# Layer 1's memory gate stored turned, its values product swapped, and the projections of the shared stage reordered

## The chip, the cores and the metric

The kernel runs on one core of one Trainium2 chip. The metric is the device time of one execution in microseconds (us); three runs of the kernel before gave 2721.72, 2722.89 and 2724.37 us, median 2722.89. The engines are named as the profile names them: PE (TensorE matmuls; PEld its weight loads), DVE (VectorE), ACT (ScalarE), POOL (GpSimd) and SP (the queue that issues most DMAs).

## What is computed

One inference step of a two-layer decoder trunk over 2048 prompt rows and 8 sample rows, all in float32 (D = 1024, four heads of 128 in every attention). Layer 0 mixes a gated short convolution with a memory attention. Layer 1 mixes a dilated window attention of three groups with a memory attention. The parts of layer 1 that the change touches:

```python
z = rms_norm(x, norm_g) @ w_in
qd, gd, mq, mg = jnp.split(z, [...])                 # 3 queries of 512, gate 512, memory query 512, memory gate 512
dil_out = dil_fn(qd).reshape(b, t, D_DIL) * jax.nn.silu(gd)
q = rms_norm(mq.reshape(b, t, MEM_HEADS, HEAD_DIM), mem_q_g) * (HEAD_DIM ** -0.5)
mem_out = mem_attend(q, mem_kv).reshape(b, t, D_MEM) * jax.nn.silu(mg)
out = jnp.concatenate([dil_out, mem_out], axis=-1) @ w_out
return x + out
```

`mem_attend` is a softmax over 256 memory rows followed by the product with the memory's values. The keys and values of the three dilation groups (`shared_kv`) are one projection of x, with a norm on the keys.

## The kernel before

Every large matrix product is made of three PE products of split operands (`split3`, lines 128 to 132: high by high, high by low, low by high), so a 128x512 result tile over eight chunks of 128 takes 24 matmuls. A transpose ("turn") is a matmul against the identity into PSUM.

The stages run in this order: the first mixing stage of layer 0 (`mix_stage`), its attention and output stage (`out_stage` with `conv` true), the projections of layer 1 (`shared_stage`), the dilated attention (`dil_stage`), and the output stage of layer 1 (`out_stage` again, `conv` false). Each engine executes its own list in order; semaphores carry the dependences. The lists are written out by hand, one function per engine.

**shared_stage** makes twelve blocks of 512 channels: key and value of three groups, three queries, the memory query, and two gates (block 4 is gd, block 5 is mg). The two blocks in `first` are made one after the other by plain products, one 128-token tile per step (lines 1455 to 1471 on PE). In the first of them ACT takes squares for the norm and DVE scales. In the second, ACT only copies the tile out of PSUM (line 1124), while ACT and DVE also make sums of x that the rest needs (`recombine`, `sums`, `sums_low`, `sums_high`). The other ten blocks are made as five pairs with seven half-size products in place of eight. Kinds of blocks: "norm" (four squares and a root on ACT, a reciprocal and four scalings on DVE), "copy" (nothing beyond DVE's addition) and "silu" (a sigmoid on ACT, a multiplication on DVE). Before, `first` is key(0), value(0), and the last pair is gate(4), gate(5). PE may run three tiles ahead of the engines that empty PSUM.

**out_stage, layer 1** works through 16 tiles of 128 tokens. In step t, PE runs: `values(t-1)` (16 products of probabilities and values), `turn_query(t)`, `right_end(t-2)` (12 matmuls), `scores(t)` (12 matmuls of 256 columns), `turn_o(t-1)`, `left(t-1)` (24 matmuls; the last 12 need the low half of the attention output, `olo_done`), sample gathers, `turn_probs(t)`, `turn_mix(t)`, `right_begin(t-1)`. The attention output comes as token rows: `gate` multiplies by the inverse row sum and by the gate in four DVE instructions (line 3543), `turn_o` transposes, ACT and DVE split the result (`high_o` line 3370, `low_o` line 3550).

DVE in step t: `joint_max(t)` (lines 3493, 3495), `query_low(t)` (3604), `gate(t-1)`, `add_right`, `maxima(t)` (3608, 3611), `weights(t)` (3508 to 3516), `low_o`, `combine(t)` (eight instructions of line 3527, one of 3531), the reciprocal `invert(t)` (3621), `add_left`, `probs_second(t)` (3630), `mix_low(t)` (3616), and in steps 3 to 10 additions for the sample rows (`join`, 2872 and 2875). ACT in step t: `group_weights(t)` (3405), `query_high(t)` (3434), a weighing of cached values for a sample row (`weigh`, 2801), `high_o`, two exponentials (3399), `weighted_sum(t)` (four instructions of 3394), two exponentials, another `weigh`, `probs_first(t)` (3361), `mix_high(t)` (3413). `weighted_sum(t)` waits for `weights(t)`, `scores(t)` for `query_low(t)`, which waits for `query_high(t)`.

Layer 0's `out_stage` has the turned form already: its gate is stored as channels by tokens, its values product gives turned rows, and the probabilities are scaled before they are transposed (line 3625).

Of the kernel before, what the change touches and what calls it, by code (L numbers as in the profile page):

```python
# [25 lines left out]
ALU = mybir.AluOpType  # L26
# [672 lines left out]
def shared_stage(core, block, stack, lead, prep, first, pairs, ops, bufs, xt_hi, xt_lo, xs, zero, spare, w_out, keys, opening):  # L699
# [22 lines left out]
    for blk in first:  # L722
        for i in range(SAMPLES):
            outs.append((blk.kind, P if i < NT else S, blk.dst[i * P:i * P + (P if i < NT else S), :], 0))
# [85 lines left out]
    with ExitStack() as st:  # L810
# [205 lines left out]
        def _(act):  # L1016
# [85 lines left out]
            for b in range(2):  # L1102
                for i in range(SAMPLES):
# [17 lines left out]
                    else:  # L1121
                        if i == 0:
                            act.wait_ge(o_done, SAMPLES)
                        act.activation(row, product, ACT.Copy).then_inc(o_done, 1)
# [47 lines left out]
        def _(dve):  # L1172
# [140 lines left out]
            for b in range(2):  # L1313
                for i in range(SAMPLES):
# [66 lines left out]
        def _(pe):  # L1381
# [61 lines left out]
            for b in range(2):  # L1443
                for i in range(SAMPLES):
# [12 lines left out]
                    for k in range(KD):  # L1457
# [4 lines left out]
                        if i == NT:  # L1462
                            sample_product(out % 4, xs[:, k, 0:LOW], wh[b].bitcast(F32)[:, k, :], k == 0, False)
                            m = sample_product(out % 4, xs[:, k, 0:LOW], wl[b].bitcast(F32)[:, k, :], False, k == KD - 1)
                        else:
# [1701 lines left out]
def out_stage(core, block, layer, src, x, y, ops_in, x_s, y_s, keys, front=None, remains=None, follow=None, closing=None):  # L3167
# [28 lines left out]
    with ExitStack() as st:  # L3196
# [20 lines left out]
        else:  # L3217
# [5 lines left out]
            def cat(low, u):  # L3223
# [4 lines left out]
                 "scored maxed biased exped inverted pturned first_done second_done summed og_done oturned ohi_done "  # L3228
                 "olo_done mhi_done mlo_done left_done right_done left_added right_added")
        (q_in0, q_in1, g_in0, g_in1, x_in0, x_in1, m_in0, m_in1, y_out0, y_out1, qturned, qhi_done, qlo_done,  # L3230
         scored, maxed, biased, exped, inverted, pturned, first_done, second_done, summed, og_done, oturned, ohi_done,
# [10 lines left out]
        if conv:  # L3242
            fresh, evened = core.sems(st, f"{tag}_fresh", "fresh evened")
            own = own + dec.sems + keys.sems + [fresh, evened]
            renewed = core.sb(st, f"{tag}_renewed", [P, 1])
# [19 lines left out]
        def _(sp):  # L3265
            def load(t):
# [20 lines left out]
                if conv:  # L3287
                    sp.dma_start(g_b[:, u, :].rearrange("p (h t) -> p h t", t=P),
                                 src["mg_t"].rearrange("(h p) t -> p h t", p=P)[:, :, rows]).then_inc(g_in[u], 16)
                else:  # L3290
                    sp.dma_start(g_b[:, u, :], src["mg"][rows, :]).then_inc(g_in[u], 16)
# [66 lines left out]
        def _(act):  # L3358
# [4 lines left out]
            def high_o(t):  # L3363
                if conv:
                    act.wait_ge(og_done, t + 1)
                    of = og[:, :].rearrange("p (h t) -> p h t", t=P)
                else:
                    act.wait_ge(oturned, t + 1)
                    of = turned_heads
# [66 lines left out]
            def step(t):  # L3436
# [3 lines left out]
                if not conv and t > 1:  # L3440
                    group_weights(t)
                if conv or t > 1:
# [45 lines left out]
        def _(dve):  # L3488
# [31 lines left out]
            def combine(t):  # L3520
                u = t % 2
                dve.wait_ge(od_begun, t + 1)
                for g in (1, 2):
# [7 lines left out]
                dve.tensor_tensor(od[:, :], od[:, :], gd_b[:, u, :], ALU.mult).then_inc(ops, 1)  # L3531

            def gate(t):
# [4 lines left out]
                if conv:  # L3538
                    dve.tensor_tensor(og[:, :], ps[:, 3, :], g_b[:, u, :], ALU.mult).then_inc(og_done, 1)
                    return  # L3540
                for h in range(H):
                    cols = slice(h * HD, (h + 1) * HD)
                    m = dve.scalar_tensor_tensor(out=og[:, cols], in0=sums[:, h, :], scalar=stat[:, 3, h:h + 1],
                                                 in1=g_b[:, u, cols], op0=ALU.mult, op1=ALU.mult)
                m.then_inc(og_done, 1)

            def low_o(t):
                dve.wait_ge(ohi_done, t + 1)
                of = og[:, :].rearrange("p (h t) -> p h t", t=P) if conv else turned_heads
# [68 lines left out]

            def invert(t):
                dve.wait_ge(exped, t + 1)  # L3620
                dve.reciprocal(stat[:, 3, :], stat[:, 2, :]).then_inc(inverted, 1)
                if conv:
                    dve.wait_ge(inverted, t + 1)
                    for h in range(H):
                        m = dve.tensor_scalar(prob[:, h, :], prob[:, h, :], stat[:, 3, h:h + 1], None, ALU.mult)
                    m.then_inc(evened, 1)
# [5 lines left out]
            def first():  # L3632
# [4 lines left out]
                else:  # L3637
                    joint_max(1)
# [8 lines left out]
            def step(t):  # L3647
# [16 lines left out]
                if not conv and t > 1:  # L3664
                    weights(t)
# [4 lines left out]
                else:  # L3670
                    combine(t)
# [43 lines left out]
        def _(pe):  # L3715
# [13 lines left out]
            def values(t):  # L3729
# [13 lines left out]

            def turn_o(t):

                pe.wait_ge(og_done, t + 1)
                turn(og).then_inc(oturned, 1)
# [21 lines left out]
            def turn_probs(t):  # L3769
                pe.wait_ge(evened if conv else exped, t + 1)  # L3770
# [43 lines left out]
            def first():  # L3814
# [9 lines left out]
                else:  # L3824
                    pe.wait_ge(mlo_done, 1)
                    project(0, 0, range(MIX))
                turn_probs(0)
# [505 lines left out]
```

## Time and profile before

| | |
|---|---|
| median of three runs | 2722.89 us (2721.72 to 2724.37) |
| the profiled execution | 2719.55 us, span 2717.4 us |
| PE busy | 2702.2 us, 99% of the span |
| DVE busy | 1789.1 us, 66% |
| ACT busy | 1112.9 us, 41% |
| chain that ended last | PE 93%, DVE 4% |
| PE clock | full in all 40 slices |
| layer 1's output stage | about 2432 to 2717 us of the span |

The span is the profiled time of the core's program; 2.2 us lie around it. "Busy" of PE counts overlapping matmuls as one stretch, so a share of 99% says that something is in the array nearly always, not how fast it runs there. A line number names the instruction's source line in the kernel.

### The profile page before, as it was taken

The numbers are of one execution on the slowest core, as the hardware profiler recorded it, in microseconds if no ns is written. First come the engines' busy times: TensorE is split into PE (matmuls) and PEld (weight loads), VectorE is DVE, ScalarE is ACT, GpSimd is POOL, SyncE is SP. The second block draws the span as 40 slices with busy tenths as digits, with TensorE's granted clock in tenths as the row PEclk, the third lists the DMA queues.
The fourth block names the chain that finished last, engine by engine and source line by source line (L and its number), as shares of the span: only waits on it lengthen the run. The fifth ranks groups of instructions, "written<-read, shape, count | busy, mean of one in ns | idle before, by whom it ended". The sixth has DMA issues, their size and how long they took to land.

```text
span 2717.4 us, 41295 instructions
## 1 busy us (share of the span) xinstructions
PE 2702.2 (99%) x14834; PEld 2259.7 (83%) x14834; DVE 1789.1 (66%) x3925; ACT 1112.9 (41%) x3346; POOL 383.1 (14%) x610
## 2 busy tenths in 40 slices
PE   9999999999999999999999999999999999999999
PEld 7788888888887888878888888888888889998887
DVE  7686766768678644435575667877674767777764
ACT  7533131212326234225434353532332349876632
POOL 0101010100101000000112032333424223210000
PEclk9999999999999999999999999999999999999999
DMA  8486555655676734324266676787768789757642
GB/s 281 143 250 208 183 167 179 207 182 171 210 246 207 222 115 156 101 97 152 94 246 228 211 268 216 274 284 264 247 237 284 262 311 330 231 177 262 217 154 82
DMA packets 292628, 567.75 MB, mean 209 GB/s; under 512 B 32432, under 2 KB 91760, under 8 KB 292424
## 3 DMA queue, kind: packets, MB, share of 16 engines
q1 hardware_dynamic: 257032, 462.31, 52.0%
q0 software_dynamic: 35392, 102.80, 10.6%
q8 instruction: 118, 1.93, 0.3%
q14 instruction: 86, 0.70, 0.1%
HBM read 432.28 MB, written 132.72 MB: 208 GB/s over the span
## 4 chain that ended last, share of the span: by engine, by line
PE 93%; DVE 4%; DMA 1%; ACT 1%; issue 1%; SPq 0%; DVEq 0%; ACTq 0%
PE ps L130 27%; PE ps L132 26%; PE ps L131 26%; PE ps L4133 2%; PE ps L3736 2%; PE ps L1385 1%; PE ps L4142 1%; PE ps L3774 1%; PE ps L3719 1%; PE ps L3035 1%; PE ps L3040 1%; PE ps L228 1%; PE ps L3130 1%; DMA a_raws<-w_mem_dram 0%; DVE a_wp L124 0%
## 5 line engine op out<-in xcount | busy, mean ns | idle before, releaser
L130 PE MATMUL ps<-b_wp,b_sring 128*128 128x512 f32 x640 | 250.5, 391 | 0.0
L131 PE MATMUL ps<-b_wp,b_sring 128*128 128x512 f32 x640 | 249.2, 389 | 0.0
L132 PE MATMUL ps<-b_wp,b_sring 128*128 128x512 f32 x640 | 249.1, 389 | 0.0
L130 PE MATMUL ps<-a_sring,a_wp 128*128 128x512 f32 x512 | 200.0, 391 | 0.0
L131 PE MATMUL ps<-a_sring,a_wp 128*128 128x512 f32 x512 | 199.3, 389 | 0.0
L132 PE MATMUL ps<-a_sring,a_wp 128*128 128x512 f32 x512 | 199.2, 389 | 0.0
L130 PE MATMUL ps<-b_wp,b_xthi 128*128 128x512 f32 x480 | 188.3, 392 | 0.0
L131 PE MATMUL ps<-b_wp,b_xthi 128*128 128x512 f32 x480 | 187.0, 389 | 0.0
L132 PE MATMUL ps<-b_wp,b_xtlo 128*128 128x512 f32 x480 | 186.7, 389 | 0.0
L1200 DVE TENSOR_TENSOR shared_o<-ps,b_spare 128x512 f32<-128x512 f32 x160 | 109.7, 685 | 112.3 <-PE ps L132 97.1
L1032 ACT ACTIVATE ps<-shared_o 128x128 f32<-128x128 f32 x390 | 103.4, 265 | 163.2 <-DVE shared_o L1200 146.0
L130 PE MATMUL ps<-a_xthi,out_cat 128*128 128x512 f32 x384 | 152.7, 398 | 0.1
L908 POOL DMA_DIRECT2D kv_dram<-shared_o x96 | 52.8, 550 | 688.8 <-DVE shared_o L1185 561.7
L132 PE MATMUL ps<-a_xthi,out_cat 128*128 128x512 f32 x384 | 149.9, 390 | 0.0
L130 PE MATMUL ps<-a_xthi,a_wp 128*128 128x512 f32 x384 | 149.8, 390 | 0.0
L131 PE MATMUL ps<-a_xtlo,out_cat 128*128 128x512 f32 x384 | 149.8, 390 | 0.0
L131 PE MATMUL ps<-a_xtlo,a_wp 128*128 128x512 f32 x384 | 149.5, 389 | 0.0
L132 PE MATMUL ps<-a_xthi,a_wp 128*128 128x512 f32 x384 | 149.5, 389 | 0.0
L130 PEld LDWEIGHTS ps<-b_wp,b_sring 128*128 128x128 f32 x640 | 120.1, 188 | 26.4 <-issue 1.2
L132 PEld LDWEIGHTS ps<-b_wp,b_sring 128*128 128x128 f32 x640 | 120.1, 188 | 25.1
L131 PEld LDWEIGHTS ps<-b_wp,b_sring 128*128 128x128 f32 x640 | 120.2, 188 | 24.4
L1185 DVE SCALAR_TENSOR_TENSOR shared_o<-shared_o,shared_stat,shared_grow 128x128 f32<-128x128 f32 x390 | 119.0, 366 | 3.6
(494 smaller groups left out, 6877.3 us busy)
## 6 DMA issues: line engine op xcount, KB each, us to landing
b_sring<-sums_dram SPq DMA_DIRECT2D x160, 512.0 KB, 5.2
a_sring<-sums_a_dram SPq DMA_DIRECT2D x128, 512.0 KB, 5.1
b_raws<-w_b_dram SPq DMA_DIRECT2D x176, 256.0 KB, 4.5
a_raws<-w_a_dram SPq DMA_DIRECT2D x140, 256.0 KB, 4.1
kv_dram<-shared_o POOLq DMA_DIRECT2D x96, 256.0 KB, 4.0
tok_b_dram<-shared_o POOLq DMA_DIRECT2D x96, 256.0 KB, 4.3
front<-tok_b_dram SPq DMA_DIRECT2D x96, 256.0 KB, 3.9
front<-grp_dram SPq DMA_DIRECT2D x48, 260.0 KB, 4.2
```

Source lines behind the costliest of these rows:

```text
L130: pe.matmul(acc, a_hi, b_hi, start=first, stop=False)
L131: pe.matmul(acc, a_hi, b_lo, start=False, stop=False)
L132: return pe.matmul(acc, a_lo, b_hi, start=False, stop=last)
L228: m = pe.transpose(self.core.ps[:, self.bank(t) + k // 4, at:at + n], self.xn[0:n, u, k * P:(k + 1) * P], self.core.ident[0:n, 0:n])
L908: pool.dma_start(dst, o[:, i % RING, :]).then_inc(o_out[i % RING], 16)
L1032: sq = act.activation(to[:, cols], of[:, cols], ACT.Square, accum_out=stat[0:n, slot, 0, h:h + 1])
L1185: m = dve.scalar_tensor_tensor(out=o[0:n, slot, cols], in0=of[:, cols], scalar=stat[0:n, slot, 2, h:h + 1], in1=grow[0:n, g, cols], op0=AL ...
L1200: dve.tensor_tensor(o[:, i % RING, :], product, with_acc, ALU.add).then_inc(o_done if kinds[i] == "copy" else added, 1)
L1385: m = pe.matmul(ps[h * LOW:(h + 1) * LOW, bank, 0:HD], x, w[:, h * HD:(h + 1) * HD], start=first, stop=last)
L3035: pe.transpose(self.query_bank(s)[:, cols], self.q_b[:, u, cols], ident[:, :])
L3736: m = pe.matmul(sums[:, h, :], of if conv else p, p if conv else of, start=(mt == 0), stop=(mt == MT - 1))
L4133: m = pe.matmul(sums_at(s)[:, h, :], pt[:, h, i, :], v_at[key % V][:, cols], start=(i == 0), stop=(i == len(order(s)) - 1))
```

## The change

1. In `shared_stage`, `first` becomes the memory query and gate(5); pairs 0 and 1 become query(0), query(1) and query(2), gate(4); key(0), value(0) move to the last pair. The second block of `first` is now made turned: weights are the stationary operand, 512 tokens the moving one, and the 128x512 results (128 channels by 512 tokens) go to a new scratch tensor. Its kind is silu, so ACT takes a sigmoid there and DVE multiplies.
2. In layer 1's `out_stage` the gate is loaded as channels by tokens. The values product swaps its operands and gives turned rows. `turn_o` goes away. `gate` is one DVE instruction.
3. A new DVE function `even` scales the four heads' probabilities before `turn_probs`, which now waits for it.
4. DVE runs `weights(t)` right behind `joint_max(t)`, and the first half of `combine` ahead of `add_right`; ACT runs `weighted_sum(t)` ahead of `query_high(t)` and the four exponentials together. PE turns the mix ahead of the probabilities (from step 2 on).

The core of the diff:

```diff
-        for i in range(SAMPLES):
-            outs.append((blk.kind, P if i < NT else S, blk.dst[i * P:i * P + (P if i < NT else S), :], 0))
+    for i in range(NT):
+        outs.append((turned_block.kind, P, turned_dst[turned_at(i)], 0))
...
-                        act.activation(row, product, ACT.Copy).then_inc(o_done, 1)
+                        act.activation(row, product, ACT.Sigmoid).then_inc(acted, 1)
...
+                        dve.wait_ge(acted, acted_at[out] + 1)
+                        row = view(o[:, out % RING, :], out)
+                        dve.tensor_tensor(row, view(ps[:, bank, :], out), row, ALU.mult).then_inc(o_done, 1)
...  ACT, step(t)
                     group_weights(t)
+                    weighted_sum(t)
                 if conv or t > 1:
                     query_high(t)
...
-                exponentials(t, (0, 1))
-                if not conv and t > 1:
-                    weighted_sum(t)
-                exponentials(t, (2, 3)).then_inc(exped, 1)
+                exponentials(t, range(H)).then_inc(exped, 1)
...  DVE
+            def even(t):
+                dve.wait_ge(inverted, t + 1)
+                for h in range(H):
+                    m = dve.tensor_scalar(prob[:, h, :], prob[:, h, :], stat[:, 3, h:h + 1], None, ALU.mult)
+                m.then_inc(evened, 1)
...  DVE, step(t)
                     joint_max(t)
+                    weights(t)
                 if t > (UNITS_UNTIL if conv else 1):
                     query_low(t)
                 if not (conv and t <= UNITS_UNTIL):
                     gate(t - 1)
+                if not conv and t > 1:
+                    combine(t, (1,))
                 if t >= 2:
                     add_right(t - 2)
...
-                if not conv and t > 1:
-                    weights(t)
...
-                    combine(t)
+                    combine(t, (2,) if t > 1 else (1, 2))
...  PE
-                        m = pe.matmul(sums[:, h, :], of if conv else p, p if conv else of, start=(mt == 0),
+                        m = pe.matmul(sums[:, h, :], of, p, start=(mt == 0),
...
-                if not conv:
-                    turn_o(t - 1)
...
+                if not conv and t > 1:
+                    turn_mix(t)
                 turn_probs(t)
-                if not conv:
+                if not conv and t == 1:
                     turn_mix(t)
...  build
-                pairs = [Pair(query(0), query(1), norm_b, 2),
-                         Pair(query(2), Block("norm", io["tok_b"][3], 7, w_of(9)), norm_b, 2),
+                first = (Block("norm", io["tok_b"][3], 7, w_of(9)), gate(5))
+                pairs = [Pair(query(0), query(1), norm_b, 2), Pair(query(2), gate(4), norm_b, 2),
                          Pair(key(1), value(1), kv_norm, 1), Pair(key(2), value(2), kv_norm, 1),
-                         Pair(gate(4), gate(5), norm_b, 2)]
+                         Pair(key(0), value(0), kv_norm, 1)]
```

## Rows read from the trace of the kernel before

**Rows 1.** The page, section 1: busy us, share of the span, instructions.
```profile
PE 2702.2 (99%) x14834; PEld 2259.7 (83%) x14834; DVE 1789.1 (66%) x3925; ACT 1112.9 (41%) x3346; POOL 383.1 (14%) x610
```
**Rows 2.** Busy time by stretch: second first block; layer 1's output tiles 2 to 4.
```profile
1338.00:1430.00 92.00, 92.00 (x519) 76.26 (x517) 65.32 (x107) 31.29 (x64) 10.68 (x20) 1.00 0.60 225
...
2450.00:2500.00 50.00, 49.99 (x294) 42.39 (x293) 35.62 (x98) 34.54 (x114) 0.00 (x0) 1.00 0.75 252
```
**Rows 3.** Timeline of PE, step 5: start, length, engine, line, out<-in.
```profile
2500.08 1.95 PE L3736 MATMUL ps<-b_spare 128*128 128x128 f32 x16
...
2505.07 0.28 PE L130 MATMUL ps<-b_xtlo 128*128 128x256 f32 x1
...
2506.51 0.60 PE L3719 MATMUL ps<-ident,front_og 128*128 128x128 f32 x4
2506.86 0.48 PE L130 MATMUL ps<-b_xthi,out_cathi 128*128 128x512 f32 x1
2507.18 0.39 PE L131 MATMUL ps<-b_xtlo,out_cathi 128*128 128x512 f32 x1
...
2513.06 1.09 PE L3774 MATMUL ps<-ident,front_prob 128*128 128x128 f32 x8
...
2517.17 1.95 PE L3736 MATMUL ps<-b_spare 128*128 128x128 f32 x16
```
**Rows 4.** Timeline of DVE and ACT, step 5 (last row: step 6's first).
```profile
2501.92 0.16 DVE L3493 TENSOR_REDUCE front_cstat<-front 128x4 f32<-128x12 f32 x1
...
2502.32 0.21 ACT L3405 ACTIVATE front_cstat<-front_cstat 128x12 f32<-128x12 f32 x1 [3.69 <-DVE front_cstat L3495]
...
2506.71 1.23 DVE L3608 TENSOR_REDUCE front_stat<-ps 128x4 f32<-128x1024 f32 x1 [0.74 <-PE ps L132]
...
2508.05 0.16 DVE L3508 TENSOR_TENSOR front_cstat<-front,front_cstat 128x12 f32<-128x12 f32 x1
...
2508.74 0.68 DVE L3550 TENSOR_TENSOR out_catlo<-ps,out_cathi 128x512 fp32r<-128x512 f32 x1
...
2509.09 1.28 ACT L3394 ACTIVATE front_od<-front,front_cstat 128x128 f32<-128x128 f32 x4
...
2510.39 2.31 DVE L3527 SCALAR_TENSOR_TENSOR front_od<-front,front_cstat,front_od 128x128 f32<-128x128 f32 x8 [0.97 <-ACT front_od L3394]
...
2514.19 0.69 DVE L3630 COPY b_spare<-ps 128x512 f32<-128x512 f32 x1
...
2514.67 0.58 ACT L3361 ACTIVATE b_spare<-ps 128x512 f32<-128x512 f32 x1
...
2519.02 0.16 DVE L3493 TENSOR_REDUCE front_cstat<-front 128x4 f32<-128x12 f32 x1
```
**Rows 5.** Timeline: values product, joint_max of steps 2, 8; joint_max of 9, 12.
```profile
2449.01 2.02 PE L3736 MATMUL ps<-b_spare 128*128 128x128 f32 x16 [0.16 <-DVE b_spare L3630]
...
2450.87 0.15 DVE L3493 TENSOR_REDUCE front_cstat<-front 128x4 f32<-128x12 f32 x1
...
2551.88 1.95 PE L3736 MATMUL ps<-b_spare 128*128 128x128 f32 x16
...
2554.36 0.15 DVE L3493 TENSOR_REDUCE front_cstat<-front 128x4 f32<-128x12 f32 x1
...
2568.95 0.16 DVE L3493 TENSOR_REDUCE front_cstat<-front 128x4 f32<-128x12 f32 x1
...
2621.58 0.15 DVE L3493 TENSOR_REDUCE front_cstat<-front 128x4 f32<-128x12 f32 x1
```
**Rows 6.** Timeline of step 1: PE turns the probabilities, DVE takes the reciprocal.
```profile
2447.09 1.03 PE L3774 MATMUL ps<-ident,front_prob 128*128 128x128 f32 x8
...
2447.53 0.16 DVE L3621 RECIPROCAL front_stat<-front_stat 128x4 f32<-128x4 f32 x1
```
**Rows 7.** Groups of DVE: the scaling of probabilities in layer 0.
```profile
L3625 DVE TENSOR_SCALAR out_prob<-out_prob,out_stat 128x256 f32<-128x256 f32 x64 | 18.3, 350 | 0.6
```
**Rows 8.** Groups of ACT: table loads ahead of the sigmoid.
```profile
L1053 ACT ACT_TABLE_LOAD x2 | 2.6, 1283 | 0.0
```

More of the change, by code:

```diff
@@ L696, in __init__, with shared_stage @@
         self.wh1, self.wl1 = prep.buffers(stack)
-def shared_stage(core, block, stack, lead, prep, first, pairs, ops, bufs, xt_hi, xt_lo, xs, zero, spare, w_out, keys, opening):
+def shared_stage(core, block, stack, lead, prep, first, turned_dst, pairs, ops, bufs, xt_hi, xt_lo, xs, zero, spare, w_out, keys, opening):
     nc, ps, io = core.nc, core.ps, core.io
@@ L721, in shared_stage @@
     outs = []
-    for blk in first:
-        for i in range(SAMPLES):
-            outs.append((blk.kind, P if i < NT else S, blk.dst[i * P:i * P + (P if i < NT else S), :], 0))
+    rows_block, turned_block = first
+    for i in range(SAMPLES):
+        n = P if i < NT else S
+        outs.append((rows_block.kind, n, rows_block.dst[i * P:i * P + n, :], 0))
+    turned_at = lambda i: (slice(i % H * P, (i % H + 1) * P), slice(i // H * C, (i // H + 1) * C))
+    for i in range(NT):
+        outs.append((turned_block.kind, P, turned_dst[turned_at(i)], 0))
+    outs.append((turned_block.kind, S, turned_block.dst[T:TS, :], 0))
     for pair in pairs:
@@ L3518, in weights, with combine @@
                                   cstat[:, 4:5, 0:H].to_broadcast([P, 3, H]), ALU.mult).then_inc(ops, 1)
-            def combine(t):
+            def combine(t, groups):
                 u = t % 2
                 dve.wait_ge(od_begun, t + 1)
-                for g in (1, 2):
+                for g in groups:
                     for h in range(H):
@@ L3537, in gate @@
                 dve.wait_ge(summed, t + 1)
[L3538 to L3545, printed above, removed]
+                dve.tensor_tensor(og[:, :], ps[:, 3, :], g_b[:, u, :], ALU.mult).then_inc(og_done, 1)
             def low_o(t):
                 dve.wait_ge(ohi_done, t + 1)
-                of = og[:, :].rearrange("p (h t) -> p h t", t=P) if conv else turned_heads
+                of = og[:, :].rearrange("p (h t) -> p h t", t=P)
                 dve.tensor_tensor(cat(1, t % 2)[:, MIX:KO, :], of, cat(0, t % 2)[:, MIX:KO, :], ALU.subtract
@@ L3621, in invert @@
                 dve.reciprocal(stat[:, 3, :], stat[:, 2, :]).then_inc(inverted, 1)
[L3622 to L3626, printed above, removed]
+                even(t)
             def probs_second(t):
@@ L3637, in first @@
                 else:
+                    even(0)
                     joint_max(1)
@@ L3826, in first @@
                     project(0, 0, range(MIX))
+                    pe.wait_ge(front.o_left, 1)
+                    project(0, 1, range(1))
                 turn_probs(0)
@@ L3830, in first @@
                 else:
-                    pe.wait_ge(front.o_left, 1)
-                    project(0, 1, range(MIX // 2))
+                    project(0, 1, range(1, MIX // 2))
                 dec_end(0)
@@ L3872, in _ @@
                 pe.wait_ge(fresh, 1)
-            if not conv:
-                pe.wait_ge(mlo_done, NT)
-                turn_o(NT - 1)
             left(NT - 1)
@@ L4250, in build @@
                 gate = lambda n: Block("silu", io["tok_b"][n], None, w_of(6 + n))
[L4251 to L4252 removed]
+                first = (Block("norm", io["tok_b"][3], 7, w_of(9)), gate(5))
+                pairs = [Pair(query(0), query(1), norm_b, 2), Pair(query(2), gate(4), norm_b, 2),
                          Pair(key(1), value(1), kv_norm, 1), Pair(key(2), value(2), kv_norm, 1),
[L4254 to L4255 removed]
+                         Pair(key(0), value(0), kv_norm, 1)]
+                tail = shared_stage(core, block, st, lead, prep, first, io["gate_b_t"], pairs, ops, bufs, xt_hi, xt_lo, xs,
                                     zero, spare, io["w_out_b"], keys, opening)
```

55 lines of the change are left out of this document (23 added, 32 removed).

## The prediction

> **What bounds the kernel.** I began with the page's busy shares: PE is busy 2702.2 of 2717.4 us [rows 1], and the chain that ended last is 93% PE. The busy time by stretch then says whether that holds in each stage that is touched. In the second first block PE fills 92.00 of 92.00 us with DVE at 65.3 and ACT at 31.3; in tiles 2 to 4 of layer 1's output stage 49.99 of 50, with DVE at 35.6 and ACT at 34.5, at full clock [rows 2]. So the time falls only by work taken from PE, and rises by each wait that PE does not have now. What counts is the slack of the waits in PE's list, read from the timeline of one step. Write V for the start of a step's values product, S for that of its scores, J for joint_max. In step 5, V = 2500.08 and S = V + 4.99; the step lasts 17.09 [rows 3]. J = V + 1.84 [rows 4].
>
> **Removed: turn_o.** Its four transposes hold PE from 2506.51 to 2506.86, 0.35 us, and the next projection is followed by its second matmul after 0.32 us where 0.23 is the usual distance, so 0.44 in all [rows 3]. It runs 16 times: -7.04 us. No other PE work goes: the swapped values product has the same sixteen 128x128x128 products. Which operand is stationary could matter; no row shows it, I bound it by 0.1 us a step either way (1.6 in all) and take 0.
>
> **Edits costed at nothing.**
> - The turned first block: the same 24 matmuls of 512 columns a tile. DVE gets one multiplication of 128x512 for each of 16 tiles, 0.68 each by low_o's [rows 4], 11 us: 65 becomes 76 of 92 us [rows 2]. ACT's sigmoid takes the place of a copy of equal size. PE runs up to three tiles ahead, so this cover holds. Without it each late tile would cost under 0.7 us.
> - The exchanged pairs: the same kinds of blocks, products and stores in another order. PE has 92.00 of 92.00 with either kind; a few table loads come to stand between other blocks (last rival).
> - The gate's load, now in rows of 128 tokens: it is issued a whole step, 17 us [rows 3], ahead by the same SP queue; SP's order and POOL's stores stay. If it landed late only DVE's gate would wait.
> - The gate on DVE: four instructions become one, a gain off the path. `even` in steps 2 to 15: four scalings take 18.3 / 16 = 1.15 us [rows 7]. Before, the transposes of probabilities waited only for the exponentials. They start at S + 7.99 [rows 3]. Now the mix's four transposes go first, and I place them at S + 7.99 - 0.44 + 0.36 + 0.17 = S + 8.08 (0.17 from low_o, below). DVE loses the second half of its old queue before the reciprocal (the weights 0.69 and half of combine 1.16 have moved ahead of it), so `even` ends near S + 7.45. It is 0.6 short of being last.
>
> **Added (a): steps 0 and 1.** Here DVE is the chain. In step 1 the reciprocal starts at 2447.53, when PE has already begun to transpose at 2447.09 [rows 6]. `even(0)` adds 1.15 to DVE's list ahead of joint_max(1); some 0.9 of it arrives at the scores (ends: 0 and 1.15). The reciprocal then starts at 2448.4, ends 0.16 later, and `even(1)` adds 1.15 and about 0.06 for the semaphore: turn_probs at 2449.8, 2.7 later than before. With step 1's own share of the removed transposes counted above, the added wait is 3.1 (ends 2.2 and 3.4).
>
> **Added (b): the query behind weighted_sum.** This is the main term. ACT now takes weighted_sum ahead of query_high, and weighted_sum waits for DVE's weights. So the scores hang on one chain from joint_max: group_weights starts at J + 0.40 and takes 0.21; weights 0.69 (2508.05 to 2508.74); weighted_sum 1.28; query_high 0.58, by the other 128x512 copy on ACT; query_low 0.68, by low_o of that shape [rows 4]; with four hand-overs of about 0.04, S is at least J + 4.0. PE has no other work between turn_query and scores than right_end, and reaches them at V + 4.99. Behind a late scores stand all matmuls of the step. So a step is late when J > V + 1.0. What sets J is DVE's end of the step before: the second probabilities, mix_low, and in steps 3 to 10 the sample joins.
> - Step 2: J = V + 1.86 before [rows 5]; the longer turned chain makes it 1.95: 0.96 late.
> - Steps 4 to 7 (step 5 stands for them): J is 5.96 after turn_probs [rows 3, 4]. 0.48 of that came from probs_first, at 2514.67 on ACT beside 2514.19 on DVE [rows 4]; with ACT's list reordered I take it away, 5.48. Then J = S + 8.08 + 5.48 = S + 13.56, while the next V is S + 12.10 - 0.44 + 0.17 = S + 11.83. So J = V + 1.73, and 0.74 late, in each of four: 3.0.
> - Step 8: J = V + 2.48 [rows 5]; the gate of a sample on DVE now also holds the shorter step, 2.82: 1.83 late.
> - Step 12: V is four steps of 17.1 after step 8's, 2620.3; J = 2621.58, V + 1.28 [rows 5]; by the shorter step 1.53: 0.54 late.
> - Steps 9 to 11 have J at V or little after it (step 9: 2568.95 beside 2551.88 + 17.1 = 2568.98 [rows 5]), with a full 1.0 of slack; 3 and 13 to 15 are like them: 0.
>
> Sum 0.96 + 3.0 + 1.83 + 0.54 = 6.3 us. Ends: 0, if ACT and DVE overlap as before, and 9.3, if the tail stays 5.96 and step 3 joins.
>
> **Added (c): low_o.** With gate, half of combine (2.31 / 2) and add_right ahead of it, maxima starts near S + 2.3 in a late step and not at S + 1.64 (2506.71 [rows 4]). low_o ends at S + 4.35, where PE wants the low half at S + 4.2. That is 0.17 in each of seven late steps, 1.2, plus 0.5 in step 3: 1.7 (ends 0 and 4).
>
> **Sum.** 3.1 + 6.3 + 1.7 - 7.04 = +4.1 us. The profiled execution took 2719.55 us, so 2723.7 beside it; the median of the runs shown is 3.34 above that execution, which makes 2727.0.
>
> **Rivals.**
> - *All hidden, -7.0:* 2715.9. It needs J before V + 1.0 in steps 4 to 7. For it: DVE has 14 us idle in 50 [rows 2], and four idle pieces could close. Against: J stands after V in these steps already, and nothing in DVE's end of a step was removed. 0.07.
> - *Only steps 0 and 1 pay, -7.04 + 3.1 = -3.9:* 2719.0. The late queries would be hidden if J came 0.8 earlier, by DVE reaching its joins before PE's turned probabilities. For it: step 9 shows a J that early with joins. Against: step 5 and 8. 0.15.
> - *Slower: the weighing of cached values holds probs_first.* In the new list of ACT the second weigh (twelve activations, some 3.5 us) stands between the exponentials and probs_first. If it ends later than turn_probs + 1.13, the tail stays 5.96; I place its end at S + 9.17 against a limit of S + 9.21, which is a tie. Then J is 0.48 later in steps 4 to 8: 5 x 0.48 = +2.4, together +6.5: 2729.4. For it: before, probs_first did start late by that much [rows 4]. 0.20.
> - *Slower: table loads.* The sigmoid now alternates with roots and exponentials in the first block and pair 1, so some four more loads of 1.28 us stand in ACT's list [rows 8]. ACT is idle two thirds of this stretch [rows 2], which is why the sum has 0. If each stopped PE for its length: 4 x 1.28 = +5.1, 2732.1. It decides only where ACT is behind by three tiles. 0.04. The Trainium skill ("ScalarE: Activation LUTs", "What ACT_TABLE_LOAD costs") puts a switch at 1283 ns for the load and some 1380 ns more for a drain; by that, as an estimate, four would be 10.6 us and the time 2737.6. The trace agrees on the load; a drain stands in no row.
>
> **How the numbers follow.** 0.2% is 5.4 us, about what a measurement of this kernel tells from no change: faster is under 2717.4, slower over 2728.3. The forecast, 2727.0, has 0.54, with its own range 2722 to 2731; about 0.15 of it is over 2728.3. Slower: 0.15 + 0.20 + 0.04 = 0.39. Faster: 0.07 and a third of the second rival's 0.15, 0.12. Within: 0.49. The range reaches from the first rival to beyond the last: 2716 to 2733.
>
> **What would show it.** Right: no L3719 on front_og; PE idle for 0.5 to 1.8 us before the scores in steps 2, 4 to 8 and 12, released by DVE's query_low; PE idle before turn_probs in step 1 released by the scaling; a step of 16.65 us in 9 to 11 and about 17.5 in 5 to 7; PE without gaps in the shared stage. Wrong: steps of 16.65 throughout (first two rivals); a J 2.2 after V in steps 4 to 7 with probs_first behind the weighing (third); PE idle beside a table load in the first block (fourth). A wait of turn_probs for `even` after step 1 would be a term that I have at nothing.

## The result, and the profile after

The changed kernel took 2731.62 us (median of 8 runs, 2729.12 to 2732.57) beside 2721.86 of the kernel before (8 runs): ratio 1.003, 95% interval 1.002 to 1.004. Run once more beside other kernels it took 2731.24 against 2721.70, ratio 1.0036 (1.0023 to 1.0048). So it is 9.5 to 9.8 us slower, 0.35 to 0.36%. The forecast was +4.1 us and 2727.0; the measured time lies inside the range of 2716 to 2733, on the slower side of the 0.2% bound, which had 0.39 against 0.49 for "within".

The profiled execution took 2729.12 us with a span of 2727.3, 9.9 more than the span before. The page of the changed kernel, section 1, answers to [rows 1]:

```profile
PE 2698.5 (99%) x14770; PEld 2251.9 (83%) x14770; DVE 1806.0 (66%) x3941; ACT 1107.2 (41%) x3330; POOL 383.2 (14%) x610
```

PE has 64 instructions less, the transposes of 16 tiles, and 3.7 us less work; yet the span grew. The list of what PE waited for (the whole span; us in total, times, longest) shows where:

```profile
PE ps L130 <- DVE b_xtlo L3599: 5.8, 7, 1.7
PE ps L130 <- DMA b_sring<-sums_dram: 3.1, 2, 2.5
PE ps L3768 <- DVE front_prob L3617: 1.7, 1, 1.7
...
PE ps L130 <- DVE shared_o L1199: 1.3, 1, 1.3
...
PE ps L130 <- DVE out_catlo L3545: 1.0, 2, 0.7
PE ps L1391 <- DMA b_raws<-w_b_dram: 0.9, 1, 0.9
PE ps L130 <- ACT dil_o L4030: 0.7, 1, 0.7
```

The first row, seven waits of the scores for query_low, and the third, the scaling ahead of turn_probs in step 1, were forecast. The waits for b_sring, for shared_o and for b_raws lie in the shared stage and were not; nor was the last row, at the start of layer 1's output stage. Of the two waits for out_catlo, which is low_o, the smaller (0.24, step 3) was forecast; the other (0.73, in step 1, where the kernel before had 0.18) was not.

Split at fixed instructions of the two timelines (the dilated stage's last values product but one, 2425.97 before and 2432.08 after; the values products that open steps 1 and 2, V1 2438.57 and 2445.39, V2 2449.01 and 2458.00; the last one, behind step 15, here called V16, 2695.14 and 2705.53; the spans' ends), the 9.9 us stand thus beside the forecast:

| stretch | forecast, us | trace, us |
|---|---|---|
| up to near the end of the dilated stage | 0 | +6.1 |
| from there to V1 | 0 | +0.7 |
| step 1 | +2.7 | +2.2 |
| steps 2 to 15 | +1.8 | +1.4 |
| from V16 to the end | -0.4 | -0.5 |
| sum | +4.1 | +9.9 |

The output stage from V1 on came within about a microsecond of the forecast. The first two lines hold 6.8 us that the forecast did not have; the five waits of PE in the shared stage (1.28, 2.53, 0.26, 0.55 and 0.92) make 5.5 of them. Step 5 after, in the order in which the chain runs (PE, DVE and ACT; answers to [rows 3, 4]):

```profile
2509.92 1.95 PE L3735 MATMUL ps<-b_spare 128*128 128x128 f32 x16
...
2511.76 0.16 DVE L3494 TENSOR_REDUCE front_cstat<-front 128x4 f32<-128x12 f32 x1
...
2513.24 1.28 ACT L3397 ACTIVATE front_od<-front,front_cstat 128x128 f32<-128x128 f32 x4 [0.86 <-DVE front_cstat L3517]
2514.43 0.57 ACT L3437 ACTIVATE b_xtlo<-ps 128x512 fp32r<-128x512 f32 x1
2515.03 0.69 DVE L3599 TENSOR_TENSOR b_xtlo<-ps,b_xtlo 128x512 fp32r<-128x512 f32 x1 [1.83 <-ACT b_xtlo L3437]
2515.78 0.39 PE L130 MATMUL ps<-b_xtlo 128*128 128x256 f32 x1 [0.70 <-DVE b_xtlo L3599]
...
2519.34 0.69 DVE L3545 TENSOR_TENSOR out_catlo<-front_og,out_cathi 128x512 fp32r<-128x512 f32 x1
...
2521.92 1.14 DVE L3617 TENSOR_SCALAR front_prob<-front_prob,front_stat 128x256 f32<-128x256 f32 x4
...
2524.07 1.04 PE L3768 MATMUL ps<-ident,front_prob 128*128 128x128 f32 x8
...
2527.68 0.27 PE L3735 MATMUL ps<-b_spare 128*128 128x128 f32 x1
```

joint_max at V + 1.84, weighted_sum, query_high, query_low, scores: the scores start at J + 4.02 = V + 5.86 where they started at V + 4.99. The step lasts 17.76 us.

In the shared stage the longest wait shows the mechanism of the last pair. First PE, then SP's queue ahead of it (start, length of the issue):

```profile
2135.33 0.47 PE L130 MATMUL ps<-b_wp,b_sring 128*128 128x512 f32 x1 [2.53 <-DMA b_sring<-sums_dram]
```
```profile
2121.95 0.32 SPq L973 DMA_DIRECT2D b_sring<-sums_dram  x1
2128.26 0.33 SPq L961 DMA_DIRECT2D b_raws<-w_b_dram  x1
2128.64 0.43 SPq L973 DMA_DIRECT2D b_sring<-sums_dram  x1
```

SP stood for 6 us at the load of a weight chunk, whose buffer DVE had not yet given back (its L1306 ended at 2128.23); the load of the sums that PE needed stood behind it. And DVE was full: the busy time in 2100 to 2120 us, in the last pair (columns: the stretch, PE, PEld, DVE, ACT, POOL, each with its count; then PE's clock, DMA share, GB/s), first of the kernel before, then of the changed one:

```profile
2100.00:2120.00 20.00, 20.00 (x145) 16.42 (x144) 16.77 (x25) 6.17 (x12) 11.82 (x18) 1.00 0.83 273
```
```profile
2100.00:2120.00 20.00, 20.00 (x145) 16.42 (x144) 19.79 (x45) 10.54 (x52) 9.44 (x13) 1.00 0.69 244
```

DVE went from 16.77 to 19.79 of 20 us. A full DVE is not enough by itself, though. Pair 3, key(2) and value(2), has the same load in the answering place of the kernel before (first row; the second is its last pair), and PE idles in neither:

```profile
1940.00:1970.00 30.00, 30.00 (x189) 24.71 (x188) 29.70 (x65) 13.82 (x67) 13.05 (x19) 1.00 0.72 248
2100.00:2130.00 30.00, 30.00 (x189) 24.71 (x188) 26.20 (x37) 8.45 (x16) 17.51 (x25) 1.00 0.88 298
```

Only the last pair also loads chunks of w_out, in the same list of SP and through the same buffers. How long SP waited there for DVE to give a buffer back (us in total, times, longest): pair 3 before (1935 to 1990 us), the last pair before, the last pair after (both 2095 to 2150 us):

```profile
SPq L956 <- DVE b_wp L1303: 8.5, 2, 5.3
```
```profile
SPq L956 <- DVE b_wp L1303: 22.6, 9, 5.5
```
```profile
SPq L961 <- DVE b_wp L1306: 28.9, 8, 6.9
```

Of these three places PE idles only in the last, where both come together. No run takes the loads of w_out away, so their part is read from this comparison; DVE's part is tested below. The timeline of DVE in the last pair, before (gate tiles) and after (key tiles):

```profile
2111.33 0.68 DVE L1196 TENSOR_TENSOR shared_o<-ps,shared_o 128x512 f32<-128x512 f32 x1
...
2115.04 0.68 DVE L1196 TENSOR_TENSOR shared_o<-ps,shared_o 128x512 f32<-128x512 f32 x1
```
```profile
2114.70 0.17 DVE L1184 RECIPROCAL shared_stat<-shared_stat 128x4 f32<-128x4 f32 x1
2114.91 1.14 DVE L1188 SCALAR_TENSOR_TENSOR shared_o<-shared_o,shared_stat,shared_grow 128x128 f32<-128x128 f32 x4
...
2116.56 0.17 DVE L1184 RECIPROCAL shared_stat<-shared_stat 128x4 f32<-128x4 f32 x1
2116.77 2.38 DVE L1188 SCALAR_TENSOR_TENSOR shared_o<-shared_o,shared_stat,shared_grow 128x128 f32<-128x128 f32 x4
```

A gate tile's second pass on DVE is one multiplication, 0.68. A key tile's is a reciprocal and four scalings, 1.3, and once 2.6. A value tile has no second pass, so over the whole pair the load hardly differs (2060 to 2210 us: DVE busy 97.76 of 150 before, 102.64 after); it is the stretches of key tiles that fill up.

### The profile page after: what moved, and what is told of

The parts are those of the page before. It is cut to its first block, busy times and chain, and to the rows that moved or that the text cites. A ratio compares the mean times of both kernels' runs of the same rounds, so it can differ in the third digit from the quotient of the medians.

```text
span 2727.3 us, 41181 instructions
## 1 busy us (share of the span) xinstructions
PE 2698.5 (99%) x14770; PEld 2251.9 (83%) x14770; DVE 1806.0 (66%) x3941; ACT 1107.2 (41%) x3330; POOL 383.2 (14%) x610
## 4 chain that ended last, share of the span: by engine, by line
PE 87%; DVE 7%; DMA 2%; ACT 2%; issue 1%; SPq 0%; POOL 0%; DVEq 0%; ACTq 0%
PE ps L130 25%; PE ps L132 25%; PE ps L131 25%; PE ps L4124 2%; PE ps L3735 1%; PE ps L4133 1%; PE ps L1391 1%; PE ps L3768 1%; PE ps L3045 1%; PE ps L3050 1%; PE ps L3718 1%; PE ps L228 1%; DVE shared_o L1188 1%; PE ps L3140 1%; DMA a_raws<-w_mem_dram 0%
## 5 line engine op out<-in xcount | busy, mean ns | idle before, releaser
L913 POOL DMA_DIRECT2D tok_b_dram<-shared_o x80 | 43.8, 548 | 645.5 <-DVE shared_o L1188 613.6
```

The lines of the kernel that those rows point to most:

```text
L913: pool.dma_start(dst, o[:, i % RING, :]).then_inc(o_out[i % RING], 16)
```

## The experiments

Three questions were open: whether the blocks' order costs the 5.5 us of waits, whether DVE is why, and whether the order of ACT's list is all that stands between the output stage and the gain. Each ratio is to runs of the kernel before on the same chip, whose median was between 2721.70 and 2722.93; a difference "under the changed kernel" is to its two medians, 2731.24 and 2731.62, which were not always taken on the same chip, so it is good to about the 1.2 us by which the medians of the kernel before differ.

### The two halves of the change alone

The new order of blocks alone:

```diff
-                        act.activation(row, product, ACT.Copy).then_inc(o_done, 1)
+                        act.activation(row, product, ACT.Sigmoid).then_inc(acted, 1)
...
+                        dve.wait_ge(acted, acted_at[out] + 1)
+                        row = view(o[:, out % RING, :], out)
+                        dve.tensor_tensor(row, view(ps[:, bank, :], out), row, ALU.mult).then_inc(o_done, 1)
...
-                tail = shared_stage(core, block, st, lead, prep, (key(0), value(0)), pairs, ops, bufs, xt_hi, xt_lo, xs,
+                first = (Block("norm", io["tok_b"][3], 7, w_of(9)), gate(5))
+                pairs = [Pair(query(0), query(1), norm_b, 2), Pair(query(2), gate(4), norm_b, 2),
+                         Pair(key(1), value(1), kv_norm, 1), Pair(key(2), value(2), kv_norm, 1),
+                         Pair(key(0), value(0), kv_norm, 1)]
+                tail = shared_stage(core, block, st, lead, prep, first, pairs, ops, bufs, xt_hi, xt_lo, xs,
```

> The kernel before with the new order of blocks alone: first blocks are memory query and gate(5), the gate still as token rows, key(0) and value(0) in the last pair; layer 1's output stage is as before. Theory A (the order of the blocks costs what the trace after shows as PE idle in the shared stage, 1.28 + 2.53 + 0.26 + 0.55 + 0.92 = 5.5 us): about 2727.4 us beside 2721.9 of before, waits of the same kind near the same matmuls, layer 1's output stage as long as before. Theory B (the prediction's: exchanging blocks costs nothing, and the waits come with the turned gate or by chance in the one profiled execution): 2721.9, within 1 us, no PE idle in the shared stage.

Measured: 2726.98 us, ratio 1.0017 (1.0008 to 1.0026), +4.1. The profile has the waits at the same places: 0.94 us at 1719.14, 2.72 at 2135.50, 0.18 at 2202.84, and layer 1's output stage is as long as before (V1 to V16 256.6 us in both). Theory A holds, with 4.1 in the medians for its 5.5; these waits come without the turned gate.

The new output stage alone (the shared stage and its blocks are those of the kernel before; the gate's source, against the change):

```diff
-            src = {"q": io["tok_b"][3], "mg": io["tok_b"][5], "mg_t": io["gate_b_t"], "gd": io["tok_b"][4], "grp": io["grp"],
+            src = {"q": io["tok_b"][3], "mg": io["tok_b"][5], "mg_t": io["tok_b"][5][0:T, :].rearrange("(c r) x -> c (r x)", r=4), "gd": io["tok_b"][4], "grp": io["grp"],
```

> The new output stage of layer 1 on the old order of blocks. The gate's values are read from the token rows as if they were stored turned, so the memory part of the output is computed from misplaced gate values; every size and transfer is that of the changed kernel. Theory A: only the output stage's own cost is left, from the trace after +3.1 us from the values product of step 1 on and +0.7 at the hand-over from the dilated stage: 3.8, about 2725.7 beside 2721.9. The prediction's sum gives +4.1, 2726.0. Theory B (all of the measured 9.8 belongs to the output stage or its loads): 2731.

Measured: 2726.20 us, ratio 1.0011 (1.0002 to 1.0020), +3.3, with no wait in the shared stage and the same waits in the output stage as in the changed kernel. That is the forecast's +4.1 within the spread. Theory B falls.

The changed kernel again, unaltered:

> The changed kernel once more, unaltered, beside the others. The blocks alone gave +4.1 and the output stage alone +3.3, together 7.4, where the change gave +9.8. Theory F (the two parts add up, and the first comparison was high within its spread): 2730.3 beside 2722.9. Theory G (they make each other worse): +9.8 again, 2732.7.

Measured: 2731.24, +9.5. The two halves give 4.1 + 3.3 = 7.4. As a difference +9.5 is nearer to theory G's 9.8 than to F's 7.4, but the intervals are 2.5 to 3.4 us wide to either side, so the medians do not decide. The traces speak for F. Up to the same product of the dilated stage the blocks alone are 6.1 us later than before (2432.10 beside 2425.97), just as the changed kernel is, with 3.84 of it in waits and some 1.4 in a fall of PE's clock behind the longest (below). From there to the end the new output stage alone takes 5.3 us longer, 1.4 of it in a step with such a fall; the changed kernel takes 3.8. The parts add up to the 9.9. In the profile of this run the wait at 1719 was 2.13 us in place of 1.28, and the clock fell behind it, which says how such pieces vary from run to run.

### Why the last pair is late

The changed kernel with the norm of key(0) left out:

```diff
-                         Pair(key(0), value(0), kv_norm, 1)]
+                         Pair(Block("copy", io["kv"][0][:, 0:C], None, w_of(0)), value(0), kv_norm, 1)]
```

> The changed kernel with key(0) of the last pair made as a plain copy: its norm (four squares and a root on ACT, a reciprocal and four scalings of 1.14 us in all on DVE for each tile) is left out, so the keys of group 0 are not normalised; stores and weights are the same. Theory A1 (DVE is late in the last pair because key tiles cost it 1.3 us where a silu tile cost 0.7, so that weights and with them SP's queue are late): the waits at about 2135 to 2145 and 2203 us go, -3.3 to -4.3, 2727.4 to 2728.3 beside 2731.6; the 1.28 us in pair 1 stays. Theory A2 (the stores of key and value, or the place of the pair, crowd the transfers): waits for the sums stay, 2731.6 within 1 us.

Measured: 2727.07, ratio 1.0016 (1.0006 to 1.0025): 4.2 to 4.6 under the changed kernel. DVE in the same stretch:

```profile
2100.00:2120.00 20.00, 20.00 (x145) 16.43 (x144) 11.20 (x18) 3.79 (x7) 12.58 (x17) 1.00 0.95 353
```

DVE is at 11.20 of 20 us, and 0.41 us is left of all the waits of the last pair, with the same stores and a higher DMA share (0.95). So DVE's load is needed for these waits, and the transfers alone do not make them; SP's wait for DVE's buffers (2095 to 2150 us) is 21.9 us in place of 28.9. Theory A1 holds and A2 falls; the wait in pair 1 stayed (1.80 us), as expected.

The other way to take load from DVE there, with nothing left out: the nine products of cached keys move to pairs 1 to 3.

```diff
-        EARLY, FOURTH = list(range(0, 2 * TP - 2, 2)), list(range(4 * TP - 1, 5 * TP - 1, 2))
+        EARLY, FOURTH = list(range(0, 3 * TP - 4, 2)), list(range(4 * TP - 1, 5 * TP - 1, 2))
```

> The changed kernel with the 9 products of cached keys that DVE sums in the last pair (0.68 us each) moved into pairs 1 to 3: 12, 14 and 14 in place of 9, 11 and 11. Nothing is left out. Theory A1 (DVE's load in the last pair makes SP's queue late): 9 x 0.68 = 6.1 us less DVE work there, the waits of 2.5 + 0.3 + 0.6 us for the sums go, and perhaps the 0.9 for the weights; -3.3 to -4.3, 2727.5 to 2728.5 beside 2731.6. Rival: the products take the slack of pairs 1 to 3 in their place, and PE idles there by as much; 2731 to 2733.

Measured: 2728.06, ratio 1.0020 (1.0011 to 1.0029): 3.2 to 3.6 lower. DVE is at 16.38 of 20 us in the stretch, near the 16.77 of before, and the waits of the last pair are down to 0.16 us. The same edit takes POOL's products of these keys away too, which lengthen some of DVE's instructions (last section); the run does not part the two. The rival has a part of it too: 1.7 us of new waits stand in pair 2, at 1814 and 1818, and 0.7 at 1883. Pairs 1 to 3 had little slack either.

Pair 1 with gate(4) as a plain copy:

```diff
-                pairs = [Pair(query(0), query(1), norm_b, 2), Pair(query(2), gate(4), norm_b, 2),
+                pairs = [Pair(query(0), query(1), norm_b, 2), Pair(query(2), Block("copy", io["tok_b"][4], None, w_of(10)), norm_b, 2),
```

> The changed kernel with gate(4) of pair 1 as a plain copy: its sigmoid and multiplication are left out, so the dilated attention's gate is not applied as it should be. Theory H (PE's wait at about 1719 us in pair 1 comes because a silu tile's bank is given back only after DVE's second pass over it, behind a late store): the wait of 1.3 us goes, 2729 beside the changed kernel. Rival: the store of the tile before is late whatever the kind, and the wait stays.

Measured: 2729.59, ratio 1.0028 (1.0018 to 1.0038), 1.7 to 2.0 lower, and no wait of PE in pair 1. So the wait belongs to the gate tile. That its PSUM bank is held until DVE's second pass is how the code reads, and the wait ended with that pass (L1199); the run does not separate it from the sigmoid itself.

### The late queries

```diff
                     group_weights(t)
-                    weighted_sum(t)
                 if conv or t > 1:
                     query_high(t)
+                if not conv and t > 1:
+                    weighted_sum(t)
+                    high_o(t - 1)
...
-                high_o(t - 1)
+                if conv or t == 1:
+                    high_o(t - 1)
```

> The changed kernel with ACT's list of layer 1 changed: query_high ahead of weighted_sum, and high_o right behind weighted_sum, ahead of the weighing of cached values. Theory C (the scores are late because query_high stands behind weighted_sum): scores come at V + 5.0 in all steps, the 5.8 us of PE idle before the scores and some 0.26 in each late step go, and steps 4 to 7 last about 16.7 in place of 17.7; -5.8 to -7.5 us, 2724 to 2726 beside 2731.6. Rival D (the list only moves the wait: low_o or the scaled probabilities are then late behind the weighing): scores at V + 5.0 but PE idle of about 0.8 a step further on, 2730 to 2732.

Measured: 2723.44 us, ratio 1.0002 (0.9993 to 1.0011): 7.8 to 8.2 below the changed kernel, a little more than expected. Step 5 of this kernel (ACT, then PE's first score):

```profile
2513.06 1.95 PE L3738 MATMUL ps<-b_spare 128*128 128x128 f32 x16
...
2515.48 0.60 ACT L3437 ACTIVATE b_xtlo<-ps 128x512 fp32r<-128x512 f32 x1
2516.37 1.28 ACT L3397 ACTIVATE front_od<-front,front_cstat 128x128 f32<-128x128 f32 x4 [0.29 <-DVE front_cstat L3520]
...
2518.05 0.28 PE L130 MATMUL ps<-b_xtlo 128*128 128x256 f32 x1
```

query_high stands at V + 2.42 again, the scores at V + 4.99 with no wait, and weighted_sum is not late for anybody. Values product to values product, from the timelines:

| steps | before | changed | query ahead |
|---|---|---|---|
| 2, 3 | 33.88 | 34.24 | 32.58 |
| 4 to 7 | 68.99 | 71.51 | 67.21 |
| 8 | 17.11 | 18.80 | 17.16 |
| 9 to 11 | 51.32 | 49.92 | 49.92 |
| 12 | 17.34 | 17.66 | 16.66 |
| 13 to 15 | 57.49 | 55.40 | 55.40 |
| sum | 246.13 | 247.53 | 238.93 |

With the query ahead, steps 2 to 15 are 7.2 us shorter than before. Rival D falls. With high_o left behind the weighing:

> The changed kernel with query_high ahead of weighted_sum on ACT, but high_o left behind the weighing of cached values. Theory C: the 5.8 us before the scores go here too. In the steps with a weighing, high_o comes at about S + 3.1 and low_o ends at S + 4.4 where PE wants it at S + 4.2, so 0.2 us a step is lost in steps 4 to 8: 2724.4, 1 us above the run with both (2723.4). If high_o's place does not matter: 2723.4.

Measured: 2722.73, ratio 1.0005 (0.9996 to 1.0015). In the trace steps 5 and 6 last 17.05 and 17.01 us in place of 16.64, so high_o's place is worth 0.4 in each of these; that is too little to be seen in the time.

The same list of ACT on the old order of blocks:

> The new output stage on the old order of blocks (gate values misplaced as in the run of the tiles alone), with query_high and high_o ahead on ACT. If the turned form is paid by the late query and by the order of the blocks, and by nothing else than some 2.9 us in steps 0 and 1: -7.2 in steps 2 to 15, +2.9, -0.5 at the end, -4.8: 2718.1 beside 2722.9.

Measured: 2717.46, ratio 0.9982 (0.9973 to 0.9991), -4.2 of the expected -4.8. So the new output stage does pay once neither the query nor the blocks take it back: in the trace 7.2 us in steps 2 to 15, about what turn_o was costed at, of which steps 0 and 1 take 2.9. This version makes no turned gate, so it shows what the stage is worth and is no kernel to use.

### Steps 0 and 1, and a version that gains

```diff
+                if not conv and t < 2:
+                    dve.tensor_copy(stat[:, 0, 0:1], stat[:, 3, 0:1]).then_inc(evened, 1)
+                    return
                 for h in range(H):
```

> The changed kernel without the four scalings of tiles 0 and 1 of layer 1 (the reciprocal stays, one small copy stands in their place), so the probabilities of these two tiles are not divided by their sums. Theory E (DVE is the chain there, the scalings stand on it): from the values product of step 1 to that of step 2 12.61 us become about 10.4 (-1.1 for each tile's four scalings), the wait of 1.7 us ahead of turn_probs goes, and the time is 2.2 lower, 2729.4 beside 2731.6. Rival: PE's wait there is for the second half of combine and the sample's probabilities, and only 0.5 goes.

Measured: 2729.12, ratio 1.0025 (1.0015 to 1.0034), 2.1 to 2.5 lower. But V1 to V2 went from 12.61 to 11.55 only, half of what was expected: the wait ahead of turn_probs fell from 1.70 to 0.68, and what is left waits for the reciprocal behind combine. Theory E had the place right and the size twice too large in the trace; the rest of the medians' difference is within their spread.

Query ahead and key products earlier, together:

> The changed kernel with both edits: query_high and high_o ahead on ACT, and the products of cached keys in pairs 1 to 3. If the two causes are independent: the 8.2 us that the first gave and the 3.3 to 4.3 of the second, 2719 to 2720.3; that is 3 us under before. If the list of transfers is late for another reason: 2723.

Measured: 2719.57, ratio 0.9988 (0.9980 to 0.9997): 3.4 us below the kernel before. The two gains add up, as two independent causes would. With step 1 rearranged as well:

```diff
-                else:
-                    combine(t, (2,) if t > 1 else (1, 2))
-                if not conv and t == 1:
-                    dec_middle(t)
+                elif t > 1:
+                    combine(t, (2,))
+                else:
+                    combine(t, (1,))
                 invert(t)
+                if not conv and t == 1:
+                    combine(t, (2,))
+                    dec_middle(t)
+                    probs_second(t)
...
                 add_left(t - 1)
-                probs_second(t)
+                if conv or t > 1:
+                    probs_second(t)
```

> Both edits, and in step 1 the scaling ahead of the second half of combine, and probs_second ahead of add_left. The scaling ends at about 1.3 us after the exponentials in place of 3.3, PE transposes the probabilities at once, and the mix 0.6 later; the values product of step 2 comes 0.8 us earlier: 2718.3 to 2719.5. Rival: the mix is then as late as the probabilities were, no difference from the run with both edits.

Measured: 2719.26, ratio 0.9987 (0.9978 to 0.9996). V1 to V2 is 11.73 in place of 12.61, as expected; a wait of 0.68 for the mix takes part of the place of the 1.70. The further 0.3 in the time can't be told from none. Of the versions that leave nothing out it is the fastest: 3.7 us, 0.13%, under the kernel before.

## Why the prediction was right or wrong, point by point

**The number: inside the range partly by luck.** The direction was worked out: the new output stage alone is 3.3 us slower. But the forecast's own range ended at 2731; the range of 2716 to 2733 reaches further only for the sake of the table loads (2732.1), which cost nothing. The time came out that high by a term that the sum had at nothing.

**Removed, turn_o: right.** -0.44 a step was forecast; steps 9 to 11, which are not late, went from 17.11 to 16.64, -0.47. Steps 13 to 15 gained 0.70 each; 0.2 of that is not explained by a wait in either trace and stays open.

**`even` hidden in steps 2 to 15: right.** In step 5 it ends at 2523.06, S + 7.28, and the transposes start at S + 8.29. PE's list has no wait for it after step 1.

**(a) steps 0 and 1: right in kind.** The reciprocal of step 1 starts after the moved work and the scaling ends last, as the forecast had it:

```profile
2454.64 0.16 DVE L3622 RECIPROCAL front_stat<-front_stat 128x4 f32<-128x4 f32 x1
2454.84 1.14 DVE L3617 TENSOR_SCALAR front_prob<-front_prob,front_stat 128x256 f32<-128x256 f32 x4
...
2456.03 1.09 PE L3768 MATMUL ps<-ident,front_prob 128*128 128x128 f32 x8 [1.70 <-DVE front_prob L3617]
```

Step 1 grew by 2.2 where 2.7 was forecast. The term that was too large is what arrives of `even(0)`: the reciprocal starts at V1 + 9.25 where it was V1 + 8.96, 0.3 later and not 0.9, and without both scalings step 1 is only 1.1 shorter, about the 1.15 of `even(1)` alone. What the forecast left out is one line of the diff: in step 0 the first piece of the next projection moved ahead of turn_probs, and with it its wait for the dilated output, 0.66 us at 2442.09, the +0.7 of the table.

**(b) the query behind weighted_sum: right, and the price within 10%.** S is J + 4.0 in the late steps, as worked out. J came at V + 1.84 in steps 5 to 7 (forecast 1.73), so 0.87 late (0.74); step 8 was 1.89 late (1.83), step 2 0.89 (0.96), step 12 0.72 (0.54). Together 6.9 us, forecast 6.3.

**(c) low_o: right.** From scores to turn_probs the changed kernel takes 1.8 us more, over all steps, than the one with the query ahead (0.16 to 0.59 in seven steps, 0.16 less in step 8); forecast 1.7.

**The edits costed at nothing: here the prediction failed.** The step is "the exchanged pairs: the same kinds of blocks, products and stores in another order. PE has 92.00 of 92.00 with either kind". The busy time that it rested on [rows 2] is that of a first block, where DVE has 65 of 92 us. The last pair is another place: DVE also splits w_out there, and had 16.77 of 20 us to begin with. There the kind decides, 0.68 a tile against 1.3, and weights come late to SP's queue and with them the sums. Blocks alone: +4.1 measured. That PE had no idle in the pairs that held keys before was no evidence: DVE is as full there, but SP's list has no w_out. The wait at 1719, in pair 1, is a second cost of the same step: a gate tile stands where a norm tile stood. The turned first block itself cost nothing, as forecast: PE has no wait in it.

**The rivals.** "All hidden" and "only steps 0 and 1 pay" fall with the seven waits. The weighing does not hold probs_first: turn_probs to joint_max is 5.45 us (2506.31 to 2511.76), the forecast had 5.48 and this rival 5.96. The table loads fall: there is one more from the shared stage on, not four, since four new ones replace three in the last pair and behind it, and PE's wait near one has another cause: the load at 1711.46 ends at 1712.74, ACT is then idle until DVE's addition, and the wait at 1719 follows DVE's own wait for a store. One of the four new ones in the blocks, with ACT's next instruction:

```profile
1781.20 1.28 ACT L1029 ACT_TABLE_LOAD   x1
1782.50 0.21 ACT L1029 ACTIVATE shared_stat<-shared_stat 128x4 f32<-128x4 f32 x1
```

The next activation starts 0.02 us behind the load. The Trainium skill ("ScalarE: Activation LUTs", "What ACT_TABLE_LOAD costs") adds some 1380 ns of drain to a switch; the trace agrees on the load's 1283 ns and shows no such drain here (the instruction ahead of the load ends at 1781.19).

## What to carry to other kernels

An edit is costed in the stretch where it lands, with all that the same engine does there and with who waits for it: that DVE had room in this stage was true of the first block and false of the last pair, and a DVE just as full in pair 3 stopped nobody. In a list that runs in order, an instruction that waits for another engine goes behind the one that PE is waiting for; moving four small activations behind one copy (with high_o) was worth 8 us, more than the whole removed transpose. And a queue that carries two kinds of loads passes the lateness of the one on to the other: PE waited for sums because weights had no buffer.

## What the runs showed of the hardware

**PE's clock fell after waits.** In the run of the new tiles alone, PE idled for 1.72 us before the scores of step 8. The stretches behind it (columns as above):

```profile
2565.40:2566.90 1.50, 1.50 (x12) 1.50 (x13) 1.50 (x5) 1.50 (x7) 0.00 (x0) 1.00 0.00 0
2567.00:2569.90 2.90, 2.90 (x8) 2.23 (x8) 2.84 (x6) 1.30 (x4) 0.00 (x0) 0.50 0.98 311
2570.40:2574.00 3.60, 3.60 (x17) 2.76 (x15) 2.21 (x8) 2.95 (x12) 0.00 (x0) 1.00 0.85 293
```

The granted clock is 0.50, the lower of its two levels (1.2 of 2.4 GHz), for eight matmuls that come 0.43 us apart in place of 0.23: 1.6 us more. The same stands in the profiles of six of the twelve runs above, each time behind an idle stretch of 1.7 to 2.8 us (in the changed kernel's second profile behind the 2.13 us at 1719). It did not follow each such wait: the first profile of the changed kernel has 2.53 us of idle at full clock. So a wait of PE can cost almost as much again; the forecast had no such term.

**DVE's instructions with both operands in SBUF took 1.2 to 1.5 us longer when POOL multiplied keys beside them.** In the last pair of the changed kernel, POOL, and DVE's two instructions beside it:

```profile
2116.90 1.30 POOL L612 TENSOR_TENSOR shared_keyrows<-shared_keyrows 128x512 f32<-128x512 f32 x1
...
2122.46 1.30 POOL L612 TENSOR_TENSOR shared_keyrows<-shared_keyrows 128x512 f32<-128x512 f32 x1
```
```profile
2122.12 2.20 DVE L1293 SCALAR_TENSOR_TENSOR b_raws<-b_raws,gains,b_n 128x512 f32<-128x512 f32 x1
```

The four scalings at 2116.77 took 2.38 in place of 1.14, and L1293, 0.74 at 2126.89, took 2.20: each about one POOL instruction of 1.30 more. The gate's multiplication in the kernel before, with one operand in PSUM, kept its 0.68 beside a POOL product at 2111.51. Once it was POOL that took longer: at 2133.67, just behind the start of an L1293 of 0.75, its product took 1.75. The Trainium skill states this rule ("SBUF — State Buffer", "Who interferes with whom"): a VectorE instruction with two SBUF inputs contends with a GpSimd instruction that reads SBUF; one with at most one does not, outside VectorE's two-port modes. The trace agrees, and it means that a norm is exposed to it where a silu is not.
